# Retention scores and state product on two row halves, next weights split two slots earlier, half tiles reordered in a hybrid decoder kernel

## The reference

```python
def retention(q, k, v):
    qc, kc, vc = chunks of 128 rows of q, k, v                    # 8 chunks a head
    decay = where(diff >= 0, exp(log_gamma * max(diff, 0)), 0)
    scores = einsum('bhncd,bhnkd->bhnck', qc, kc) * decay
    o_inner = einsum('bhnck,bhnkv->bhncv', scores, vc)
    xi, zeta = exp(log_gamma * (i + 1)), exp(log_gamma * (C - 1 - i))
    kz = kc * zeta
    def step(R, inp):
        q_n, kz_n, v_n = inp
        o = einsum('bhcd,bhdv->bhcv', q_n, R)
        R = R * chunk_decay + einsum('bhcd,bhcv->bhdv', kz_n, v_n)
        return R, o
    o_cross = scan(step, 0, ...) * xi
    return o_inner + o_cross

# in even_mixer: rope on q and k before it, group norm over v behind it, then silu(gate) * output
# in swa_mixer: banded attention of width 128, then its output @ w_out
```

## Time and profile before

| | |
|---|---|
| median of 3 runs | 2354.9 us (2354.2 to 2355.9) |
| profiled execution, own time | 2353.9 us |
| its span | 2352.1 us |
| PE busy | 2296.8 us, 98% of the span |
| DVE, POOL, ACT busy | 61%, 47%, 36% |
| granted TensorE clock, mean | 0.998 |

### The profile page before, as it was taken

One profiled execution on the slowest core, in us unless ns is written; L12 is line 12 of the kernel. 1 busy time (PEld: TensorE's weight loads), 2 busy tenths in 40 slices (PEclk: granted clock), 3 DMA queues, 4 the chain that ended last, 5 costly groups with the idle time before them and its releaser, 6 DMA issues.

```text
span 2352.1 us, 34850 instructions
## 1 busy us (share of the span) xinstructions
PE 2296.8 (98%) x12280; PEld 1922.1 (82%) x12280; DVE 1446.2 (61%) x2862; ACT 840.1 (36%) x1797; POOL 1100.4 (47%) x994
## 2 busy tenths in 40 slices
PE   6999999999999999999999999999999999999999
PEld 5787878789978888888887777779978888888887
DVE  7565646472476667577664676662476667577664
ACT  5535253531332223233223555552332223233220
POOL 5323332322284566467465543332284566467461
PEclk9999999999999999999999999999999999999999
DMA  3101111122102110210213011013102110210211
GB/s 128 30 26 28 28 28 28 28 72 86 54 19 72 63 62 18 71 54 27 80 36 113 33 31 32 21 48 104 54 19 72 63 62 18 71 54 29 79 36 72
DMA packets 140983, 120.38 MB, mean 51 GB/s; under 512 B 26048, under 2 KB 126912, under 8 KB 140864
## 3 DMA queue, kind: packets, MB, share of 16 engines
q1 hardware_dynamic: 133488, 103.70, 14.2%
q10 hardware_dynamic: 7376, 15.12, 1.9%
HBM read 110.41 MB, written 8.39 MB: 51 GB/s over the span
## 4 chain that ended last, share of the span: by engine, by line
PE 85%; DVE 7%; ACT 3%; issue 2%; POOL 2%; DMA 1%; SPq 0%; DVEq 0%; ACTq 0%; POOLq 0%
PE gp L489 13%; PE gp L491 13%; PE gp L490 13%; PE sc L491 6%; PE sc L489 6%; PE sc L490 6%; PE tp L490 2%; PE tp L491 2%; PE tp L489 2%; PE sc L552 2%; PE sc L596 1%; PE tp L561 1%; PE qt L489 1%; PE qt L491 1%; PE o_ps L489 1%
## 5 line engine op out<-in xcount | busy, mean ns | idle before, releaser
L489 PE MATMUL gp<-W_hi,hT_hi 128*128 128x384 f32 (+1 forms) x1152 | 415.8, 361 | 5.4 <-POOL W_lo L1855 5.4
L491 PE MATMUL gp<-W_hi,hT_lo 128*128 128x384 f32 (+1 forms) x1152 | 383.9, 333 | 0.0
L490 PE MATMUL gp<-W_lo,hT_hi 128*128 128x384 f32 (+1 forms) x1152 | 382.5, 332 | 0.0
L1980 POOL TENSOR_TENSOR W_lo<-af,W_hi 128x512 fp32r<-128x512 f32 x168 | 237.8, 1415 | 282.7 <-ACT W_hi L1133 282.7
L1960 POOL TENSOR_TENSOR W_lo<-raw,W_hi 128x1024 fp32r<-128x1024 f32 x72 | 187.4, 2608 | 230.8 <-ACT W_hi L1075 217.9
L1674 DVE TENSOR_TENSOR af<-af 128x512 f32<-128x512 f32 x112 | 81.2, 725 | 300.5 <-ACT af L1116 300.5
L489 PEld LDWEIGHTS gp<-W_hi,hT_hi 128*128 128x128 f32 x1152 | 219.1, 190 | 34.3 <-issue 25.1
L1980 POOL TENSOR_TENSOR W_lo<-rb,W_hi 128x512 fp32r<-128x512 f32 x168 | 243.8, 1452 | 0.0
L490 PEld LDWEIGHTS gp<-W_lo,hT_hi 128*128 128x128 f32 x1152 | 219.4, 190 | 0.0
L491 PEld LDWEIGHTS gp<-W_hi,hT_lo 128*128 128x128 f32 x1152 | 218.0, 189 | 0.0
L489 PE MATMUL gp<-hT_hi,W_hi 128*128 128x512 f32 x512 | 199.7, 390 | 0.0
(11 more groups left out here) (306 smaller groups left out, 5275.8 us busy)
## 6 DMA issues: line engine op xcount, KB each, us to landing
raw<-in_mlp_w_up SPq DMA_DIRECT2D x64, 512.0 KB, 4.2
rb<-in_mlp_w_down SPq DMA_DIRECT2D x56, 512.0 KB, 5.0
raw<-in_hyb_w_in SPq DMA_DIRECT2D x74, 128.0 KB, 2.4
X<-in_x SPq DMA_DIRECT2D x8, 512.0 KB, 7.3
X<-in_x ACTq DMA_DIRECT2D x8, 512.0 KB, 3.5
raw<-in_mlp_w_down SPq DMA_DIRECT2D x8, 512.0 KB, 3.3
raw<-in_swa_w_qkv SPq DMA_DIRECT2D x16, 256.0 KB, 3.1
x_spill<-X ACTq DMA_DIRECT2D x8, 512.0 KB, 2.8
```

The lines of the kernel that those rows point to most:

```text
L489: mm(o, a[0], b[0], start=first, stop=False)
L490: mm(o, a[0], b[1], start=False, stop=False)
L491: return mm(o, a[1], b[0], start=False, stop=last)
L1980: E.tensor_tensor(WF_lo[:, c], x(k), WF_hi[:, c].bitcast(f32), ALU.subtract).then_inc(op_ready, 1)
```

## The change

1. The rotated query and key now both go to tile QK in the order key, query, query times xi, key times zeta; tile rQK is gone. The key is turned by one transpose onto rows 0 to 63, and query and query times xi together by a second one onto rows 0 to 63 and 64 to 127. ACT copies the two turned tiles (256 columns, all rows) in place of three (384 columns, 64 rows). The state rR lives on rows 64 to 127.
2. `ret_scores` issues the product of the query with the state (before in `ret_values`) directly behind the scores, on the other 64 rows. It opens the output bank, and `ret_values` adds to it. For that it waits for r_x: chunks 1 and 2 for the chunk before, later ones for two chunks back. The output of chunks 3, 5 and 7 goes to bank o_ps, of the others to sc.
3. Waits for the shared tiles: `ret_rope` of chunk 0 for the attention's last transposes, POOL's `gains` in the first slots of a round for r_st, the first attention scores and values of a round for r_x and r_R.
4. `D_SPLIT_AT`: the next round's weights are split in slots 8 to 11, before in 10 to 13.
5. End of stage 2: ACT does `heads_T_copy` before `copy_half` of the second half; DVE does `prep` before `lo_half` of the first half, and `lo_half` of the second half in the next slot, behind `outputs`.

```diff
-        D_SPLIT_AT = {4: 0, 5: 1, 6: 2, 7: 3, 10: 0, 11: 1, 12: 2, 13: 3}
+        D_SPLIT_AT = {4: 0, 5: 1, 6: 2, 7: 3, 8: 0, 9: 1, 10: 2, 11: 3}
+        LO, HI = slice(0, HD), slice(HD, 2 * HD)
-        r_add = sc[0:HD, P:P + RV]
-        r_out = sc[:, 512:512 + RV]
+        r_add = sc[HI, P:P + RV]
+        r_outs = [o_ps[:, 0:RV] if r in (3, 5, 7) else sc[:, 512:512 + RV] for r in range(T)]
...
@@ part_scores, part_values
-                        pe.wait_ge(r_x, g * T)
+                        pe.wait_ge(r_x, g * T - 1)
+                        pe.wait_ge(r_R, g * T)
...
+                if a == 0 and g > 0:
+                    pe.wait_ge(r_x, g * T)
...
@@ ret_T
-                q, k, qx = rQK[:, r % 2, 0:HD], rQK[:, r % 2, HD:2 * HD], QK[:, r % 2, 4 * HD:5 * HD]
-                for m, src in enumerate((q, k, qx)):
-                    last = nc.tensor.transpose(qt[0:HD, m * P:(m + 1) * P], src, ident[:, :])
-                last.then_inc(r_qt, 1)
+                nc.tensor.transpose(qt[LO, 0:P], QK[:, r % 2, 0:HD], ident[:, :])
+                nc.tensor.transpose(qt[:, P:2 * P], QK[:, r % 2, HD:3 * HD], ident[:, :]).then_inc(r_qt, 1)
@@ ret_scores
+                else:
+                    pe.wait_ge(r_x, n if r <= 2 else n - 1)
+                    pe.wait_ge(r_R, n)
+                if r == 3:
+                    pe.wait_ge(ot_copied, (g + 1) * T)
                 pe.wait_ge(r_qtev, n + 1)
-                mm(sc[:, 0:P], rqT[:, 1, :], rqT[:, 0, :], start=True, stop=True)
-                mm(r_add, QK[:, r % 2, 5 * HD:6 * HD], v, start=True, stop=True).then_inc(r_st, 1)
+                mm(sc[:, 0:P], rqT[LO, 0, :], rqT[LO, 1, :], start=True, stop=True)
+                if r >= 1:
+                    mm(r_outs[r], rqT[HI, 1, :], rR[HI, r % 2, :], start=True, stop=False)
+                mm(r_add, QK[:, r % 2, 3 * HD:4 * HD], v, start=True, stop=True).then_inc(r_st, 1)
@@ ret_values
-                if r >= 1:
-                    pe.wait_ge(r_x, n)
-                o = r_out
-                last = mm(o, rsT[:, :], G[:, r % RING, 2 * HD:2 * HD + RV], start=True, stop=(r == 0))
-                if r >= 1:
-                    pe.wait_ge(r_R, n)
-                    last = mm(o, rqT[:, 2, :], rR[:, r % 2, :], start=False, stop=True)
-                last.then_inc(r_o, 1)
+                mm(r_outs[r], rsT[:, :], G[:, r % RING, 2 * HD:2 * HD + RV], start=(r == 0), stop=True).then_inc(r_o, 1)
@@ ACT, s_slots
-                        if t >= O1_T:
-                            copy_half(t - O1_T, j)
-                            if j == 1:
-                                reload(t - O1_T, spill)
+                        if t >= O1_T and j == 0:
+                            copy_half(t - O1_T, 0)
...
+                        if t >= O1_T and j == 1:
+                            copy_half(t - O1_T, 1)
+                            reload(t - O1_T, spill)
@@ DVE, ret_rope
+                if r == 0:
+                    dve.wait_ge(qt_done, n + T)
@@ DVE, s_slots
+                        if j == 0 and t > O1_T:
+                            lo_half(t - 1 - O1_T, 1)
...
-                        if t >= O1_T:
-                            lo_half(t - O1_T, j)
                         if j == 0 and 0 <= t - 1 < units // 2:
                             prep("S", t - 1, A_S)
+                        if t >= O1_T and j == 0:
+                            lo_half(t - O1_T, 0)
+                lo_half(O1_HALVES - 1, 1)
@@ POOL, gains
+                elif kind == "D" and a0 > 0:
+                    pool.wait_ge(r_st, a0 - 2 + t)
```

More of the change, by code:

```diff
@@ L162, in hybrid_trunk @@
         rsT = at("rsT", [P, P])
-        rR = at("rR", [HD, 2, RV])
+        rR = at("rR", [P, 2, RV])
         rsg = at("rsg", [P, 2, RV])
         re = at("re", [P, 2, RV])
-        rQK = at("rQK", [P, 2, 2 * HD])
-        rqT = at("rqT", [HD, 3, P])
+        rqT = at("rqT", [P, 2, P])
         off[0] = A0
@@ L392, in load_R @@
                 v = 2 * RH * HD
-                runs(w_in[0], [(0, HD, h * HD), (HD, HD, RH * HD + h * HD), (2 * HD, RV, v + h * RV),
+                runs(w_in[0], [(0, HD, RH * HD + h * HD), (HD, HD, h * HD), (2 * HD, RV, v + h * RV),
                                (2 * HD + RV, RV, v + RH * RV + h * RV)], first)
@@ L939, in ret_T_copy @@
                 act.wait_ge(r_qt, n + 1)
-                A(rqT[:, :, :].rearrange("p m c -> p (m c)"), qt[0:HD, 0:3 * P], ACT.Copy).then_inc(r_qtev, 1)
+                A(rqT[:, :, :].rearrange("p m c -> p (m c)"), qt[:, 0:2 * P], ACT.Copy).then_inc(r_qtev, 1)
             def part_probs_T(g, a, c):
@@ L1426, in ret_rope @@
                 step.wait()
-                q = rQK[:, r % 2, :]
-                step.did(E.tensor_tensor(q, rA, rB, ALU.add))
+                k, q, qx, kz = [QK[:, r % 2, m * HD:(m + 1) * HD] for m in range(4)]
+                step.did(E.tensor_tensor(QK[:, r % 2, 0:2 * HD], rA, rB, ALU.add))
                 step.wait()
-                step.did(E.tensor_scalar(QK[:, r % 2, 4 * HD:5 * HD], q[:, 0:HD], xi[:, bass.ds(h, 1)], None, ALU.mult))
-                E.tensor_scalar(QK[:, r % 2, 5 * HD:6 * HD], q[:, HD:2 * HD], zeta[:, bass.ds(h, 1)], None,
-                                ALU.mult).then_inc(r_qk, 1)
+                step.did(E.tensor_scalar(qx, q, xi[:, bass.ds(h, 1)], None, ALU.mult))
+                E.tensor_scalar(kz, k, zeta[:, bass.ds(h, 1)], None, ALU.mult).then_inc(r_qk, 1)
                 dve.wait_ge(r_exp, n + 1)
@@ L1447, in ret_state @@
                                 ALU.mult).then_inc(r_sT, 1)
-                new = rR[:, (r + 1) % 2, :]
+                new = rR[HI, (r + 1) % 2, :]
                 if r == 0:
@@ L1452, in ret_state @@
                     dve.wait_ge(r_R, n)
-                    E.scalar_tensor_tensor(new, rR[:, r % 2, :], cdec[0:HD, bass.ds(h, 1)], r_add,
+                    E.scalar_tensor_tensor(new, rR[HI, r % 2, :], cdec[HI, bass.ds(h, 1)], r_add,
                                            ALU.mult, ALU.add).then_inc(r_R, 1)
@@ L1457, in ret_out @@
                 dve.wait_ge(r_o, n + 1)
-                step.did(E.bn_stats(bst, r_out))
+                step.did(E.bn_stats(bst, r_outs[r]))
                 step.wait()
@@ L1462, in ret_out @@
                 dve.wait_ge(r_rstd, n + 1)
-                step.did(E.tensor_scalar(rA, r_out, bag[:, 0:1], bag[:, 2:3], ALU.subtract, ALU.mult))
+                step.did(E.tensor_scalar(rA, r_outs[r], bag[:, 0:1], bag[:, 2:3], ALU.subtract, ALU.mult))
                 step.wait()
```

## The result

The changed kernel takes 2360.0 us (median of 19 runs, 2356.5 to 2364.7) where the kernel before takes 2355.7 (median of 19, 2354.2 to 2358.7): a ratio of 1.0017, 95% interval 1.0011 to 1.0024. It is slower by 4.3 us; forecast were 15.2 us less, with 2332.5 to 2347.5 as the range. So the forecast had the wrong sign, by some 20 us.

A forecast was written before the change was run, and what follows sets the result against it. TensorE, busy 98% of the span, was taken as the bound. Terms of -15.0 (retention chunks), +6.0 (splits in slots 8 to 11) and -6.2 (end of stage 2) gave -15.2: 2339.7 us, range 2332.5 to 2347.5.

The forecast's parts named there:

- slot 8: Stage 1: the split catches the attention heads' rotation, but DVE's 1.57 us wait for PE just covers it: 0.
- the free second half of the row pair: Retention chunks: the state product beside the scores on the other 64 rows costs 0, so 0.50 us per chunk goes.
- the wait on r_x: Chunk 2's scores: PE waits 1.4 us for DVE's last product of chunk 1, four times; score 0.6 later than before.
- the port stall in slot 9: Chunk 0's rotation is caught under GpSimd's split, so PE starts later: 1.5 us per round, +6.0 in four rounds.
- part 4: End of stage 2: PE's stops in slots 31 and 32 go, 4.7 us, and the low clock behind them, 1.5: -6.2.
- PE's share of the new slot: Retention chunks: a plain PE slot goes from 6.33 to 5.72 us, less 0.50 for the state product and 0.11 for one transpose.
- slots 10 to 18 of three rounds: Stage 1 retention chunks: shorter slots less chunk 2's wait, 3.75 us earlier per round; -15.0 over all four rounds.
- So the slot becomes 5.75, by both engines.: Retention chunks: PE needs 5.72 us and DVE 5.73 from one decay product to the next, so slots take 5.75.
- The other new waits ... I count 0.: Waits r_st on GpSimd, ot_copied in chunk 3, qt_done before chunk 0: for work a slot or more back, 0.
- The fourth round ... I count it like the others.: Stage 1, fourth round: it also carries the transposes of X, yet was given the same gain, 3.75 us.
- Rival B: Slot 9: the longer stop, 2.5 us, lowers the granted clock, 1.5 us per round: 2345.7 us; chance 0.12.
- rival E: Slot 8's split not covered: GpSimd holds DVE in slots 8 and 9, low clock after each: 2360.1 us; chance 0.03.

The follow-up runs named there:

- e4: Changed kernel with the halves exchanged, scores on rows 64 to 127, state and its product on rows 0 to 63: 2349.9 us, ratio 0.9979.
- e10: Changed kernel with slot 9's split later, halves exchanged, chunk 2's output in tp (rounds 1 to 3), chunk 7's statistics ahead of prep: 2335.9 us.
- e2: Kernel before with only the splits of the next weights moved to slots 8 to 11: 2363.6 us, ratio 1.0024.
- both repairs: Changed kernel with slot 9's split behind ACT's copy of the retention's transposes and the state on rows 0 to 63: 2342.5 us, ratio 0.9930.

## Why the prediction was wrong

What was right: slot 8 (9.87 for 9.84: covered), the free second half of the row pair, the wait on r_x (1.6 us for 1.4), the port stall in slot 9 (1.6 for 1.5) and part 4. PE's share of the new slot, 5.72, was right too: e4 reaches it. Wrong were these steps, against the profiled executions (8.0 us longer span; the forecast had 15.2 less, so 23.2 to explain). The lag is that of ACT's copies in stage 1 and of PE's GEMM matmuls behind it:

| step | forecast | measured |
|---|---|---|
| slot 9, four rounds | +6.0 | +13.4 (3.1, 3.0, 4.2, 3.1) |
| slots 10 to 18 of three rounds | -11.2 | -2.4 |
| slots 10 to 15 of the fourth | -3.8 | -1.2 |
| slots 31 and 32, stage 2 | -6.2 | -6.5 |
| elsewhere | 0 | +4.7 |

1. "So the slot becomes 5.75, by both engines." DVE's cycle was taken from the earlier trace rows as if only its instructions' count mattered. The state update had moved to other partitions, and it and two instructions behind it each lose 0.10 to 0.13 us. This is the largest error of understanding: 0.36 in a slot in which both engines had no slack, 2.25 per round with slots 12, 17 and 18 (e4). The price was in no row of the kernel before, whose DVE instructions of the retention all start at partition 0.
2. "The other new waits ... I count 0." The wait that cost is none of the three named there. When PE's slots become as short as DVE's cycle, DVE arrives at the end of the round behind PE, and chunk 7's last product holds the buffer sq that ACT needs: slot 18 is longer by 1.0 to 1.2 in three rounds. e10 shows it. No wait in the diff says so; the buffer is shared in the kernel before too, where the product ends at 164.11, before ACT's squares are due at 164.51.
3. "The fourth round ... I count it like the others." There slots 14 and 15 take 8.04 and 7.45 before, 7.46 and 7.45 with the splits moved alone (e2), 7.35 with the change and 7.38 with both repairs: the 0.6 us less on PE brought 0.1, DVE's 0.36 nothing. The turning of X adds 1.23 us of DVE (line 1401) and 1.09 us of PE (line 501) to each of these slots; which of the two holds them was not tested. Slot 11 also became longer there by 1.0 us (10.41 to 11.37), since the new wait of chunk 2's scores falls into it. The round gained 1.2 us.
4. Rival B had 0.12. Its mechanism came true in all four rounds of the profile, at 1.4 to 1.5 us and once at 2.6. The evidence weighed against it, one stop of 2.33 us without a low clock, was one draw: e2 shows that the same stop of 2.6 us is followed by it in some rounds and not in others. It should have been given a half, with its price. That rival E's 2360.1 lies on the measured time is coincidence: its condition, a split in slot 8 that isn't covered, did not come.

Elsewhere: +1.8 in slots 1 and 2 of the first round, with a low clock at 44.5 us that some of the kernels' profiles have and others don't; +1.1 at the end of stage 1, where the clock is low at 549.7; +1.5 in stage 2 before slot 31, of which 1.4 comes between 1484 and 1503, behind slot 20, where GpSimd's split now catches a product of two columns:

```profile
1490.40 1.81 DVE L1564 TENSOR_TENSOR st<-st 128x2 f32<-128x2 f32 x1
```

In the kernel before, with the two engines a few tenths apart from this, it catches line 1551 there, for 0.68. That this catch makes the 1.4 was not tested by itself. The rest is small: +0.6 behind stage 2, -0.3 in slot 7 of the second round. Why the first two clock falls come and go was not tested, so the cause of these 4.7 us stays in part open.

## What to carry to other kernels

When operands move to other partitions, recount DVE's sequence as well as PE's: with no slack, each switch of the starting partition on input or output, here between 0 and 64, takes the overlap with the instruction in front. A GpSimd instruction that reads SBUF should be placed where VectorE idles, not only where its own engine has time; here that place was 2.7 us later in the same slot and worth 13 us. And a stop of PE is to be priced with the low clock that may follow it.

## What was new about the hardware

- A VectorE instruction with two SBUF inputs that begins with GpSimd's split ends with it: 0.22 us became 1.85, a product of two columns 1.81.
- Starting partition 64 instead of 0 for the state update: it and two later instructions lose 0.10 to 0.13 us of overlap each, together 0.36 per chunk.
- The score and the state product on the two row halves start 0.01 us apart, though they share neither operands nor banks: the second costs nothing.
- At a stop of 2.5 to 2.65 us the granted clock fell to 0.5 in 8 cases of 12, seven times for 3.4 us and once for 6.8, at 1.2 to 1.7 us each by the length of slot 9 and once at 2.6; with the stop filled down to 1.2 us by idle transposes it did not fall (4 rounds of 4).
